# A fused decoder trunk: the decay sums of the delta-rule layer brought to all partitions by a transfer from DRAM, in place of TensorE's transposes

## What is computed

```python
def gated_delta(q, k, v, g, beta, S0):
    ...
    gc = jnp.cumsum(to_chunks(g, C, N), axis=-1)          # the decay sums
    diff = gc[..., :, None] - gc[..., None, :]
    decay = jnp.where(tri, jnp.exp(jnp.where(tri, diff, 0.0)), 0.0)
    lmat = jnp.where(strict, jnp.einsum('nbhik,nbhjk->nbhij', kb, kc) * decay, 0.0)
    ...                                                    # unit triangular solve of lmat: u, w
    aqk = jnp.einsum('nbhik,nbhjk->nbhij', qc, kc) * decay
    def step(S, xs):
        v_new = u_i - jnp.einsum('bhck,bhkv->bhcv', w_i, S)
        o_i = jnp.einsum('bhck,bhkv->bhcv', qg_i, S) + jnp.einsum('bhij,bhjv->bhiv', aqk_i, v_new)
        S = S * jnp.exp(gl_i)[..., None, None] + jnp.einsum('bhck,bhcv->bhkv', kdec_i, v_new)
        return S, o_i
```

## Time and profile before

| | |
|---|---|
| time, median of 3 runs (lowest to highest) | 2113.65 us (2112.19 to 2114.21) |
| the profiled execution: its time / its span | 2113.68 / 2111.6 us |
| TensorE's granted clock over the span | 0.993 of 2.4 GHz |
| busy: PE / DVE / ACT / POOL | 98% / 47% / 33% / 22% |
| layer B's prompt part | from about 1060 to 1670 us of the span |
| a stage of it (L2559 at 1227.85 and 1262.14) | 34.3 us |

### The profile page before, as it was taken

One profiled execution on the slowest core, in us unless ns is written; L12 is line 12 of the kernel. 1 busy time (PEld: TensorE's weight loads), 2 busy tenths in 40 slices (PEclk: granted clock), 3 DMA queues, 4 the chain that ended last, 5 costly groups with the idle time before them and its releaser, 6 DMA issues. The chain is left out here.

```text
span 2111.6 us, 36594 instructions
## 1 busy us (share of the span) xinstructions
PE 2072.5 (98%) x14446; PEld 1487.2 (70%) x14446; DVE 997.2 (47%) x2664; ACT 697.7 (33%) x1631; POOL 454.6 (22%) x639
## 2 busy tenths in 40 slices
PE   8999999999999999999999999999999999999998
PEld 6888888888888887555466777767666666665444
DVE  5234354354435345331238777777876133332252
ACT  4121321322131122231135555555564344532101
POOL 0522232222223213300023134322331200020000
PEclk9999999999999999999999999999998999999999
DMA  7411301211131127668412122222210461134451
GB/s 235 161 43 41 107 27 51 80 41 43 41 97 37 50 83 223 237 202 255 131 31 74 73 95 83 93 87 82 73 48 13 137 256 31 41 105 134 134 161 50
DMA packets 210238, 210.34 MB, mean 100 GB/s; under 512 B 14261, under 2 KB 181653, under 8 KB 209150
## 3 DMA queue, kind: packets, MB, share of 16 engines
q1 hardware_dynamic: 198070, 148.27, 23.7%
q0 software_dynamic: 12000, 59.73, 7.4%
HBM read 179.56 MB, written 68.23 MB: 117 GB/s over the span
## 5 line engine op out<-in xcount | busy, mean ns | idle before, releaser
L887 PE MATMUL bank<-arena 128*128 128x256 f32 (+1 forms) x2688 | 631.7, 386 | 0.0
L887 PEld LDWEIGHTS bank<-arena 128*128 128x128 f32 x2688 | 494.5, 190 | 75.3
L2104 PE MATMUL bank<-arena 128*128 128x352 f32 x1296 | 452.5, 470 | 0.1
L2104 PEld LDWEIGHTS bank<-arena 128*128 128x128 f32 x1296 | 220.8, 191 | 71.4 <-issue 1.0
L2909 PE MATMUL bank<-arena 128*128 128x352 f32 x576 | 176.4, 459 | 0.0
L3399 PE MATMUL bank<-arena 128*128 128x512 f32 x360 | 167.5, 599 | 0.0
L2162 PEld LDWEIGHTS bank<-arena 128*128 128x128 f32 x864 | 129.9, 194 | 45.7 <-DVE arena L2646 3.7
L2909 PEld LDWEIGHTS bank<-arena 128*128 128x128 f32 x576 | 106.6, 190 | 53.3
L1341 POOL TENSOR_TENSOR arena<-arena 128x272 f32<-128x272 f32 (+1 forms) x48 | 31.5, 656 | 507.4 <-ACT arena L1061 487.4
L2162 PE MATMUL bank<-arena 128*128 128x128 f32 x864 | 135.0, 280 | 1.5 <-DVE arena L2646 1.0
L1323 POOL TENSOR_TENSOR arena<-arena 128x512 f32<-128x512 f32 x96 | 122.8, 1279 | 11.3 <-POOL arena L1323 0.9
(11 more groups left out here) (432 smaller groups left out, 2754.1 us busy)
## 6 DMA issues: line engine op xcount, KB each, us to landing
arena<-in_w_in_a SPq DMA_DIRECT2D x48, 512.0 KB, 5.2
arena<-in_w_in_b SPq DMA_DIRECT2D x40, 512.0 KB, 7.5
arena<-in_cache_win_k SPq DMA_DIRECT2D x48, 256.0 KB, 6.1
arena<-in_cache_win_v SPq DMA_DIRECT2D x48, 256.0 KB, 4.7
out<-arena SPq DMA_DIRECT2D x40, 256.0 KB, 3.4
arena<-in_w_mem_kv SPq DMA_DIRECT2D x16, 512.0 KB, 8.1
arena<-in_cache_mem_k SPq DMA_DIRECT2D x32, 256.0 KB, 4.3
arena<-in_cache_mem_v SPq DMA_DIRECT2D x32, 256.0 KB, 4.2
```

Of the source, the lines that this page charges most:

```text
L887: m = nc.tensor.matmul(o[:, 0:hi - lo], w, y, start=k == 0 and i in (0, 1, 3, 5), stop=k == KH - 1, skip_group_check=i in (2, 4, 6))
L2104: m = nc.tensor.matmul(bank[j % 3][:, 0:PART], ring.slots[:, (B1 + b) % RING, k, :], part_in(k, part_), start=k == 0, stop=k == KD - 1)
```

## The change

Of group 0 all stays. Behind its `ra` TensorE makes one more transpose, `gr`, of `gc[:, 0:64]` (64 rows of 128), DVE copies it to SBUF, and SP stores it in DRAM (`gc_kept`, 32 KB). For the groups 1 to 15 the four transposes `ra` are gone. SP loads the four rows of the group, repeated on 128 partitions, into `ATs[g % 3]` (256 KB in pieces of 512 bytes), and DVE adds the mask in place, in slot 6 in place of 5, ahead of `chunk_step`; ACT's `exps` waits for that. SP's program is written in stages: the rows of group G+1, issued when group G-2 has had its last `av` (slot 14 of stage G-1) and the rows before have landed; then in an odd G two weight blocks, in an even G one.  The other edits give the semaphores of `Chain` back at a phase's end.

```diff
@@ constants and the list of work
-    PREP = {5: ("ra",), 7: ("kt",), 8: ("kk",), 9: ("qk",), 15: ("vt",)}
-    NEXT = ("ra", "kk", "qk")
+    PREP = {7: ("kt",), 8: ("kk",), 9: ("qk",), 15: ("vt",)}
+    NEXT = ("kk", "qk")
+    AT_MASK = 6
...
-    work = [(0, "ss"), (0, "ra"), (0, "kk"), (0, "qk")]
+    work = [(0, "ss"), (0, "ra"), (0, "gr"), (0, "kk"), (0, "qk")]
@@ SP
-        for b in range(3 * HB):
+        def rows_to(g):
+
+            h, c0 = g // 2, GR[g % 2][0]
+            if g > 2:
+                left(sp, g - 3, f"av{GR[(g - 3) % 2][1] - 1}")
+            sp.wait_ge(rows_away, 16)
+            if g > 1:
+                sp.wait_ge(rows_in, 16 * (g - 1))
+            src = gc_kept.rearrange("(c h) i -> h c i", h=HB)[h, c0:c0 + 4]
+            sp.dma_start(ATs[g % 3], src.unsqueeze(0).to_broadcast([P, 4, P])).then_inc(rows_in, 16)
+
+        def weights(b):
+
             if b % 3 == 2 and b // 3 >= 3:
                 state_away(b // 3 - 3)
             ring.load(sp, B1 + b + 1)
-        state_away(HB - 3)
-        ring.load(sp, B2 + RING)
+
+        for b in range(7):
+            weights(b)
+        readout(sp, 0, "gr")
+        sp.dma_start(gc_kept, gc_rows).then_inc(rows_away, 16)
+        for G in range(NG_):
+            if G + 1 < NG_:
+                rows_to(G + 1)
+            if G % 2 and G < NG_ - 1:
+                weights(3 * (G // 2) + 8)
+                weights(3 * (G // 2) + 9)
+            if G % 2 == 0:
+                weights(3 * (G // 2) + 7)
@@ TensorE, group 0 only
+            o = bank_free(0, "gr")
+            nc.tensor.transpose(o[0:64, 0:P], gc[:, 0:64], ident).then_inc(wk, 1)
@@ ACT, exps(G)
-            readout(act, G, "ra")
+            if G:
+                act.wait_ge(masked, G)
+            else:
+                readout(act, 0, "ra")
@@ DVE
+        def mask_rows(G):
+
+            dve.wait_ge(rows_in, 16 * G)
+            nc.vector.tensor_tensor(ATs[G % 3], ATs[G % 3], wide4(mat(M_GE)), ALU.add).then_inc(masked, 1)
...
+                if s == AT_MASK and G + 1 < NG_:
+                    mask_rows(G + 1)
```

More of the change, by code:

```diff
@@ L115, with __init__ @@
 class Chain:
-    def __init__(self, nc, eng, name):
-        self.eng, self.sem, self.n = eng, nc.alloc_semaphore(name), 0
+    def __init__(self, sem, eng, name):
+        self.eng, self.sem, self.n = eng, sem(name), 0
     def __call__(self, ins):
@@ L158, in build @@
     part = dram("part", [2, SEQ, OW])
+    gc_kept = dram("gc_kept", [64, P])
     memT_kept = dram("memT_kept", [P, KD * NMEM])
@@ L525, in _ @@
     def _(dve):
-        own = Chain(nc, dve, "in_dve")
+        own = Chain(sem, dve, "in_dve")
         def norm(n):
@@ L1130, in _ @@
     def _(dve):
-        own = Chain(nc, dve, "dve_a")
+        own = Chain(sem, dve, "dve_a")
         def evacuate(t, i):
@@ L1300, in _ @@
     def _(pool):
-        own = Chain(nc, pool, "pool_a")
+        own = Chain(sem, pool, "pool_a")
         def weight_sums(pair, ns):
@@ L1747, in _ @@
     def _(dve):
-        own = Chain(nc, dve, "wa_dve")
+        own = Chain(sem, dve, "wa_dve")
         def add(n, half):
@@ L1914, in build @@
     S = take(2, P)
+    gc_rows = r_sb[0:64, 1, :]
     S_of = lambda h, c: S3[(NT * h + c) % 3]
@@ L2000, in build @@
     (pd, pr_, wk, rd_act, rd_dve, cvd, sild, sqd, hdv, hda, exd, mt0, onm, sqo, fac, tails, sqrt_o, cstep, xzero,
-     cvs, spread, base, tap, chosen) = (
+     cvs, spread, base, tap, chosen, rows_away, rows_in, masked) = (
         sem(f"b_{n}") for n in (
@@ L2005, in build @@
             "out_factors", "conv_tails", "out_roots", "conv_steps", "buffers_zeroed", "samples_convolved",
-            "diagonals_spread", "base_steps", "first_taps", "blocks_chosen"))
+            "diagonals_spread", "base_steps", "first_taps", "blocks_chosen",
+            "rows_kept", "rows_loaded", "rows_masked"))
     s_out = stored["state"]
@@ L2214, in chunk_step, with decay_rows @@
                 to(g, f"su{c}", [(kdec[:, c, :], vn[:, c % 2, :])])
+        def decay_rows():
+            o = bank_free(0, "gr")
+            nc.tensor.transpose(o[0:64, 0:P], gc[:, 0:64], ident).then_inc(wk, 1)
         def turned(G, name):
@@ L2283, in _ @@
         turned(0, "ra")
+        decay_rows()
         for u in units[PER_HEAD + KD:PER_HEAD + 2 * KD]:
@@ L2489, in _ @@
     def _(dve):
-        own = Chain(nc, dve, "b_dve")
+        own = Chain(sem, dve, "b_dve")
         stepped = [0]
@@ L2571, in turned, with decay_rows @@
                                         .to_broadcast([P, 4, P]), ALU.mult).then_inc(rd_dve, 1)
+        def decay_rows():
+            b = left(dve, 0, "gr")
+            nc.vector.tensor_copy(gc_rows, b[0:64, 0:P]).then_inc(rd_dve, 1)
+        def mask_rows(G):
+            dve.wait_ge(rows_in, 16 * G)
+            nc.vector.tensor_tensor(ATs[G % 3], ATs[G % 3], wide4(mat(M_GE)), ALU.add).then_inc(masked, 1)
         def matrix_step(G, s):
@@ L2772, in _ @@
     def _(pool):
-        own = Chain(nc, pool, "b_pool")
+        own = Chain(sem, pool, "b_pool")
         def prefix(h, i):
@@ L3009, in _ @@
     def _(dve):
-        own = Chain(nc, dve, "m_dve")
+        own = Chain(sem, dve, "m_dve")
         def conv_turned(t):
@@ L3487, in _ @@
     def _(act):
-        own = Chain(nc, act, "d_act_own")
+        own = Chain(sem, act, "d_act_own")
         def squared(o):
@@ L3558, in _ @@
     def _(dve):
-        own = Chain(nc, dve, "wb_dve")
+        own = Chain(sem, dve, "wb_dve")
         gt2 = lambda v: v[:, 64:66].unsqueeze(2)
```

## The result

The changed kernel takes **2150.64 us** (median of 4 runs, 2146.28 to 2152.16) against 2112.92 us for the kernel before beside it: a ratio of 1.0175, 95% interval 1.0157 to 1.0192. It is slower, as predicted, but by 38 us and not by 152. The forecast of 2266 us was wrong; the first rival, 2149 us, is what happened.

A forecast was written before the change was run, and what follows sets the result against it. PE was taken to bound the kernel, except in stage 13, where DVE is late. 2113.7 - 6.0 (transposes) + 134.5 (five odd groups) + 3.5 (group 13) + 20.4 (clock) = 2266.1 us, 7.2% slower; range 2145 to 2298.

The forecast's parts named there:

- the first rival: Odd groups' rows pass ahead of the new even copy but are held by the copy before: 2149 us, chance 0.12.
- 6.0 us for the transposes: PE, stages 0 to 12 and 14: fourteen groups each lose 0.43 us of `ra` transposes, 6.0 us less.
- The mask from SBUF at 0.68 us: DVE's 128x512 mask operation, read from SBUF alone, takes the same 0.68 us as with one source in PSUM.
- The rows' issue and its place beside the copy's: Group 5's rows are issued in slot 14 of stage 3, 0.2 us ahead of stage 4's even copy.
- Odd groups, against the even copy: Stages 4, 6, 8, 10 and 2: even copy holds the rows 43.4 us; PE loses 5 x 26.9 = 134.5 us.
- should be quick: The 256 KB rows transfer: a weight block twice as large landed in 3.8 us while nothing else ran.
- the rows are slow in themselves: Rival: all partitions read the same 2 KB, a transfer taking over 10 us by itself; about 2320 us, chance 0.06.
- Only the copy before holds the rows: Rival: odd groups stand behind a weight block; six PE waits of 3.5 us, 20.4 of clock; 2149 us, chance 0.12.
- group 13: Stage 12: rows stand behind a weight block held by stage 11's odd copy; DVE stands 4.4 us, PE 3.5.
- Even groups, group 1 and group 15 cost nothing: Even copy ends 8 to 10 us after even groups' issue, mask at 15.8; groups 1 and 15 meet no copy.
- The clock, 3.4 us a wait: Behind each of six PE waits, granted clock 0.66 over 10 us loses 3.4 us; 20.4 us in all.
- Nothing holds them: Rival: engines take many small packets per large one, so rows land before the mask at 1263.2; 2107.7 us, chance 0.12.

The follow-up runs named there:

- the only-odd kernel: The changed kernel with only POOL's six copies of the odd stages (1, 3, .. 11), the even ones left out: 2154.14 us, ratio 1.0193.
- The kernel with the copy ahead: The changed kernel with POOL's copies of the even stages 2 to 10 issued between its two squares, 1.04 us earlier: 2251.99 us, ratio 1.0664.
- a held half: From the changed kernel with each group's rows loaded by two 128 KB transfers, the second issued behind the even copy: 2258.7 us, ratio 1.0692.

## Why the prediction was wrong, point by point

- **What bounds the kernel**: right. PE is the bound up to stage 12, and of DVE's wait of 4.91 us PE loses 3.97.
- **6.0 us for the transposes**: right in size. The exchange without copies gives 7.1, of which up to 3.4 may be clock in stage 13. That DVE's chain sets the end there is still so (the earlier trace rows has a wait of 1.7 us for the take-over of `x6`, and the trace after has one too), but the low stretch behind it is shorter. I had left that out.
- **The mask from SBUF at 0.68 us**: right, 649 to 694 ns, median 662.
- **The rows' issue and its place beside the copy's**: right, 0.22 us ahead of it (forecast 0.2).
- **The failed step: "Odd groups, against the even copy"**, the term of 134.5 us (five waits of PE of 26.9). The five waits measured 4.0 to 5.5 us each, 24.0 together, and the odd copy makes them. The step took the 1.4 us from the copy's issue to its first large piece as a constant, and asked only how many of the rows' pieces would pass in that time. But the earlier trace rows is a stretch in which no transfer of small pieces ran ahead of the copy. Behind a running transfer of rows the copy starts after 4.75 us (3.9 to 5.4), and behind half of one after 3.0 (1.4 to 4.0). By 1255.2 all but the pieces on the odd copy's engines have gone, or nearly. The forecast had the rows 0.75 us short of slipping through; the rows themselves moved the copy's start by 3.3 us. That the copy's own first, small pieces take turns with the rows' would be the way in which this works: the changed trace has 106 pieces of the copy's queue in the 3.8 us behind its issue where the kernel before has 208 within 1.9 us. That is argued; shown is that the start moves with the amount of rows ahead.
- **A transfer of rows "should be quick"**: half wrong. Alone it takes 4.9 us for 256 KB, against 3.8 for a weight block twice as large. Whether a quicker transfer would have kept the copy back as long is not shown. The rival "the rows are slow in themselves" wanted over 10 us for one alone; the nine that no odd copy holds cost nothing.
- **"Only the copy before holds the rows" (2149 us, chance 0.12)**: this held. Its mechanism, worked out for group 13, is that of all six odd groups. Its sizes: six waits of PE of 3.5 us, 21.0; measured 28.1, since the rows land 20.8 to 22.3 us after their issue, where its figures give 19.9. Its clock, 20.4 us, came to 11.8 in the traced execution and to an estimated 17 in the median one, since only the part above the 10.3 us that are lost anyway counts. The two errors pull against each other, so that 2149 is so close to 2150.6 is in part luck.
- **Even groups, group 1 and group 15 cost nothing**: right (nine masks without a wait).
- **The clock, 3.4 us a wait**: right for five of six (0.66 over 10 us), 1.7 for the sixth. What the sum left out is that some of it was lost before the change too, 10.3 us in layer B.
- **"Nothing holds them"**: its time, 2107.7, is near what the kernels without odd copies take (2104.1 and 2105.2), but its mechanism (many small pieces for each large one) is refuted by the only-odd kernel: rows that meet large pieces wait for the end of them.
- **The prices of being held**: 134.5 us for five waits, and 3.5 for a sixth, were near as a price. The kernel with the copy ahead lost 129.6 us in six waits of PE and took 2252; the forecast's 2266 describes it, and not the one that was to be forecast.

The chance was the second fault. Two queues whose issues stand 0.2 us apart, with a margin of 0.75 us, and no row of the trace that shows the two started together, doesn't bear 0.60.

## What to carry to other kernels

Before a transfer is put in front of a busy engine, look for long transfers with few large pieces that run beside it: each of its engines holds a part of every 16-engine transfer to its own end. Spread such a copy (16 as the slowest dimension) and move its issue away from that of the transfer that someone waits for; the spreading cost nothing in the kernel before, and the two turned 38 us of loss into 7 to 9 of gain. And where a forecast hangs on which of two queues' transfers comes first, a start time read from a stretch in which the other was absent is no evidence.

## What the runs showed of the hardware that was not expected

- The start of POOL's DRAM-to-DRAM copy depends on what is ahead: first large pieces 1.4 to 1.6 us after its issue with no rows ahead, 1.4 to 4.0 behind 256 pieces of 512 bytes, 3.9 to 5.4 behind 512.
- A read of the same 2 KB by all 128 partitions runs at some 80 GB/s and takes 4.9 us for 256 KB, the only transfer then; a weight block, with distinct addresses, runs at about 300. From 1108.0, in slices of 0.15 us:

```profile
GB/s 0 0 0 0 0 0 0 41 96 89 82 89 89 82 68 14 0 75 89 82 92 92 79 82 85 79 79 82 79 99 116 0 0 0 0 0 0 0 0 0
```

- An issue on SP's queue can itself stand. It takes 0.37 us as a rule. In the changed kernel one for the rows took 4.0 us, and behind a held half:

```profile
1271.00 0.37 SPq L2092 DMA_DIRECT2D arena<-gc_kept  x1
1272.26 14.93 SPq L2095 DMA_DIRECT2D arena<-gc_kept  x1
```

- The copies over 16 engines land in 8.6 to 9.6 us in place of 42, and cost the kernel before nothing (1.0003).
